# A hybrid decoder layer: plain last iteration of the down projection, own places for the last h forms, and queries split at another unit

## The chip, the cores and the metric

The kernel runs on one core of one Trainium2 chip. The metric is the device time of one execution in microseconds (us). The program is launched once, all inputs lie in device memory (HBM) when the time starts, and the output is written back to it.

## What is computed

One decoder layer on 512 tokens of width 2048, in fp32. Cut to what matters here:

```python
h = rms_norm(x, g_mix_pre);  proj = h @ w_in
c_q, c_kv, k_r, sq, sk, sv = split(proj)       # 512, 512, 64, 1024, 128, 128
out_a = mla_attention(...)                     # 8 heads, dense causal
out_b = swa_attention(sq, sk, sv, sinks, bias) # 16 heads of 64, window 128, 2 key heads
x = x + rms_norm(concat(out_a, out_b) @ w_o, g_mix_post)
h = rms_norm(x, g_ffn_pre)
ff = (silu(h @ w_gate) * (h @ w_up)) @ w_down  # d_ff = 5632
x = x + rms_norm(ff, g_ffn_post)
```

## The kernel before

**Split operands.** Every fp32 product is made of three matmuls: an operand a is split into a rounded high part (written by ScalarE as an activation with Copy) and a low part (VectorE: the source minus the high part), and a·b becomes hi·hi + hi·lo + lo·hi, accumulated in PSUM. So each operand costs ScalarE one pass and VectorE one pass before TensorE may start.

**Order of the work.** The engines follow lists written out by hand, with semaphore waits; nothing is reordered at run time. The stages are the input projection, sliding-window attention in 16 units (four groups of four heads, four query blocks each), latent attention, output projection, gate and up projection in 11 rounds, down projection in 12 iterations, and the last norm and residual.

**Sliding-window units.** In each `window(s)` TensorE does the scores of unit s, the transposes of unit s-3 and the values of unit s-4. The queries of head group g are split into `qs[g % 2]`: ScalarE in `split_queries_hi` (line 907), VectorE in `split_queries_lo` (line 1414). For groups 2 and 3 the two halves are done in units 1 and 2 of the group before on ScalarE (line 941), and one step after that on VectorE (line 1455: at the ends of windows 6, 7 and 10, 11). TensorE waits for both halves in front of the scores of windows 8 and 12 (line 2004).

**Strassen-Winograd.** Gate/up and down projection are done with 7 products in place of 8 for each 2x2 block. In the down projection an iteration is one chunk of the inner dimension (2, 4, 4, 4, 4, 4 pairs of 128 rows) and one half (`cb`) of each output block. Product n = 7·it + f_ takes the weight form `weights_form(f_)` (sums made in place by VectorE, line 1801), a ring slot n % 4 for its high and low part (lines 1237 and 1828), and the h form f_. With 4 pairs it is 2·4·3 = 24 matmuls, with 2 pairs 12. Its 128x1024 result in PSUM pair (n + 1) % 4 is copied (n < 14, line 1242) or added by VectorE (line 1840) into the accumulator `y[f_]`. ScalarE's `form_hi(n)` waits for product n-4, because of the ring.

**The h forms.** The activations h of a round are transposed and summed into 7 forms. Each form is split into a staging place (`h_stage`, two places used in turn; lines 1171 and 1736) and stored to `h_forms` in HBM (line 672), from where `fetch_h` (lines 662 and 666) loads them by chunk. A place is free again when its store has landed (line 1170). The forms of round 10, the last one, are made during products 5 to 12 of the down projection.

```python
if m >= 2:
    act.wait_ge(h_out[m % 2], 16 * (m // 2))              # 1170, ScalarE
nc.scalar.activation(h_stage[m % 2][:, :, 0, :], h_source(i), ACT.Copy)
```

**SP's queue.** All loads and stores of this stage are issued by SP in one order: weights after `d_lo`, h stores after `h_lo`, h loads after `d_done` (lines 721 to 750).

**The end.** In the last two iterations (10 and 11) the seven accumulators of a half are combined: GpSimd adds y0 to y5, y0 to y2, y2 to y1, y1 to y4 and y2 to y6 (`add_into`, line 823), and VectorE adds twice (lines 1845 and 1847), waiting for GpSimd. ScalarE squares the four output blocks (line 1249), VectorE multiplies by the gain (line 1856). After the last product VectorE adds it row block by row block (`late_piece`, line 1921), then for rows 0-1, 2 and 3 forms the inverse root (`y_rstd`, lines 1332 to 1336 and 1895), and adds to x1: the first half by VectorE (line 1912), most of the second by ScalarE's scale (line 1287) and GpSimd's add (line 842). SP stores the rows (lines 755 to 759).

Of the kernel before, what the change touches and what calls it, by code (L numbers as in the profile page):

```python
# [31 lines left out]
ALU = mybir.AluOpType  # L32
# [84 lines left out]
def build(nc, x, positions, g_mix_pre, w_in, g_cq, g_ckv, w_uq, w_ukv, sinks, rel_bias, w_o,  # L117
          g_mix_post, g_ffn_pre, w_gate, w_up, w_down, g_ffn_post, buckets, inv_freq, out):
    ctx = ExitStack()
    with ctx:  # L120
# [111 lines left out]
        h_stage = [sb(f"h_stage{i}", kb, [P, 2, 2, 256], F32R) for i, kb in enumerate((48, 214))]  # L232
        xs = [sb(f"xs{i}", kb, [P, 2, 512]) for i, kb in enumerate((48, 214))]
# [13 lines left out]
        g_row = sb("g_row", 142, [P, D])  # L247
# [8 lines left out]
        h_forms = nc.dram_tensor("h_forms", (7, P, FF_PAIRS, 512), F32, kind="Internal").ap()  # L256
        x1_dram = nc.dram_tensor("x1_dram", (TB, P, D), F32, kind="Internal").ap()
# [22 lines left out]
        y_pool = sem("y_pool")  # L280
# [17 lines left out]
        h_out = [sem(f"h_out{i}") for i in range(2)]  # L298
        slot_in = [[sem(f"w{i}{h}_in") for h in "ab"] for i in range(3)]
# [17 lines left out]
        h_in = [sem(f"h_in{f}") for f in range(7)]  # L317
        g_row_in = sem("g_row_in")
# [3 lines left out]
        d_first = sem("d_first")  # L322
# [5 lines left out]
        y_based = sem("y_based")  # L328
        y_mixed = sem("y_mixed")
        y_sq = sem("y_sq")  # L330
        y_scaled = sem("y_scaled")
# [174 lines left out]
        PRODUCTS = 7 * ITERS  # L506
# [27 lines left out]
        def y_part(t, half):  # L534

            return ((y[5], y[4]), (y[6], y[3]))[t // 2][half][:, t % 2, :]

# [46 lines left out]

        def h_source(i):

            return (h_s34[:, :, :], ht[:, 2, :, :], h_s2[:, :, :], ht[:, 3, :, :], ht[:, 1, :, :], ht[:, 0, :, :],
                    h_s34[:, :, :])[i]
# [19 lines left out]
        def _(sp_):  # L608
# [41 lines left out]
            def forms_stored(pairs):  # L650
                forms = 7 * ((pairs + 1) // 2)
                sp_.wait_ge(h_out[0], 16 * ((forms + 1) // 2))
                sp_.wait_ge(h_out[1], 16 * (forms // 2))

# [14 lines left out]
            def store_form(b, i):  # L669
                m = 7 * b + i  # L670
                sp_.wait_ge(h_lo, m + 1)
                sp_.dma_start(h_forms[H_FORM[i], :, 2 * b:2 * b + 2, :],
                              f(h_stage[m % 2][:, :, :, :]).rearrange("p j h n -> p j (h n)")
                              ).then_inc(h_out[m % 2], 16)
# [14 lines left out]
            for b in range(ROUNDS):  # L689
                for f_ in range(7):  # L690
                    for v in range(4):
                        if v % 2 and f_ in (3, 4, 5, 6):
# [3 lines left out]
                            elif b + 1 < ROUNDS:  # L696
# [5 lines left out]
                                else:  # L702
                                    load(b + 1, "b22", v // 2)
                        if b and (f_, v) in STORE_AT:
# [16 lines left out]
            for n in range(PRODUCTS + 3):  # L721
# [13 lines left out]
                elif it + 1 == ITERS and f_ in (1, 3, 4, 5):  # L735
                    sp_.wait_ge(d_lo, n + 1)
                    t = (1, 3, 4, 5).index(f_)
                    sp_.dma_start(x1_row[t][:, :], x1_dram[t]).then_inc(x1_in[t], 16)
                elif it + 1 == ITERS and f_ == 2:
                    sp_.wait_ge(d_done, PRODUCTS - 6)  # L740
                    sp_.dma_start(g_row[:, :], g_ffn_post.broadcast_to([P, D])).then_inc(g_row_in, 16)
# [6 lines left out]
                if done >= 0 and done // 7 % 2 and done // 14 + 1 < len(CHUNKS):  # L748
                    sp_.wait_ge(d_done, done + 1)
                    fetch_h(done // 14 + 1, done % 7)  # L750

            for t in range(TB):
                sp_.wait_ge(y_ready, t + 1)
                w = shared(t).stop
                sp_.dma_start(out_v[t][:, 0:1024], x1_row[t][:, 0:1024]).then_inc(y_out, 16)
                if w < 1024:
                    sp_.dma_start(out_v[t][:, 1024 + w:D], x1_row[t][:, 1024 + w:D]).then_inc(y_out, 16)
                sp_.wait_ge(y_pool, t + 1)
                sp_.dma_start(out_v[t][:, 1024:1024 + w], x1_row[t][:, 1024:1024 + w]).then_inc(y_out, 16)
            sp_.wait_ge(y_out, 16 * (2 * TB + 1))  # L760
# [1599 lines left out]
```

## Time and profile before

| | |
|---|---|
| time before, median of 3 runs | 2010.66 us (2010.12 to 2011.25) |
| the profiled execution's own time | 2008.88 us |
| its span, first to last instruction | 2007.1 us |
| mean granted TensorE clock | 0.976 |
| TensorE busy / VectorE / ScalarE / GpSimd | 95% / 75% / 45% / 5% |

The span is the traced part of an execution; the 1.78 us around it are not traced. TensorE is busy nearly all the time, so the stretches in which it waits are what can be won.

### The profile page before, as it was taken

The page shows a single profiled execution, that of the slowest core. Times are in us where ns is not written, and L with a number is a line of the kernel's source. Part 1 is how long each engine was busy: PE and PEld are TensorE (multiplying, and loading weights), DVE is VectorE, ACT ScalarE, POOL GpSimd, SP SyncE. Part 2 cuts the span into 40 slices and gives each one's busy share as a digit, 9 for nine tenths or more (in the row PEclk, how much of TensorE's full clock was granted, in tenths as well). Part 3 has the DMA queues.
Part 4 walks back from the last instruction along what each step waited for, and adds up shares of the span by engine and source line. Part 5 has one row for each costly group of instructions (what it writes and reads, how often), then busy time and mean ns, then how long its engine had stood idle before and what let it go on. Part 6 is the DMA issues. An engine that isn't in the chain of part 4 may idle for free. (4 is left out here: it accounts for less than half of the span.)

```text
span 2007.1 us, 22078 instructions
## 1 busy us (share of the span) xinstructions
PE 1901.0 (95%) x8706; PEld 1573.9 (78%) x8706; DVE 1504.6 (75%) x1623; ACT 900.7 (45%) x1212; POOL 109.3 (5%) x63
## 2 busy tenths in 40 slices
PE   8999989999995799999999999999999899999994
PEld 6888778888884688888888888888887688888873
DVE  5762576663226878988988888889887788888887
ACT  5322474453225644454544545545545533333332
POOL 1110130000002000000000000000000000000034
PEclk9999999999997899999999999999999999999997
DMA  8433201115413153462552642733715854644732
GB/s 241 123 97 93 84 12 58 58 64 189 147 64 126 43 168 97 145 220 92 171 180 93 209 147 101 236 116 126 241 64 210 327 219 172 258 183 174 271 125 105
DMA packets 194388, 293.32 MB, mean 146 GB/s; under 512 B 7187, under 2 KB 140396, under 8 KB 188524
## 3 DMA queue, kind: packets, MB, share of 16 engines
q1 hardware_dynamic: 191248, 285.24, 41.7%
q10 hardware_dynamic: 3036, 6.66, 1.1%
q8 instruction: 69, 1.13, 0.2%
q14 instruction: 35, 0.29, 0.0%
HBM read 243.09 MB, written 51.93 MB: 147 GB/s over the span
## 5 line engine op out<-in xcount | busy, mean ns | idle before, releaser
L2277 PE MATMUL pair<-unit_hi,xf 128*128 128x512 f32 x1232 | 488.6, 397 | 24.8 <-DVE unit_lo L1672 24.8
L2279 PE MATMUL pair<-unit_hi,xf 128*128 128x512 f32 x1232 | 483.5, 392 | 0.0
L2278 PE MATMUL pair<-unit_lo,xf 128*128 128x512 f32 x1232 | 483.3, 392 | 0.0
L2277 PEld LDWEIGHTS pair<-unit_hi,xf 128*128 128x128 f32 x1232 | 233.8, 190 | 73.6 <-issue 23.4
L2279 PEld LDWEIGHTS pair<-unit_hi,xf 128*128 128x128 f32 x1232 | 233.6, 190 | 49.9
L2278 PEld LDWEIGHTS pair<-unit_lo,xf 128*128 128x128 f32 x1232 | 234.2, 190 | 47.7
L2331 PE MATMUL pair<-ring_hi,hfs 128*128 128x512 f32 x528 | 207.1, 392 | 7.9 <-DVE ring_lo L1828 7.1
L2332 PE MATMUL pair<-ring_lo,hfs 128*128 128x512 f32 x528 | 206.4, 391 | 0.0
L2333 PE MATMUL pair<-ring_hi,hfs 128*128 128x512 f32 x528 | 206.4, 391 | 0.0
L446 DVE TENSOR_TENSOR wlo<-raw,whi 128x2048 fp32r<-128x2048 f32 (+2 forms) x47 | 96.7, 2064 | 111.0 <-ACT whi L439 111.0
L439 ACT ACTIVATE whi<-raw 128x2048 fp32r<-128x2048 f32 (+2 forms) x47 | 80.9, 1729 | 181.5 <-PE pair L602 173.0
L1237 ACT ACTIVATE ring_hi<-w_b 128x2048 fp32r<-128x2048 f32 (+1 forms) x60 | 105.3, 1772 | 124.7 <-DVE w_b L1808 56.5
L1828 DVE TENSOR_TENSOR ring_lo<-w_b,ring_hi 128x2048 fp32r<-128x2048 f32 (+1 forms) x60 | 132.1, 2202 | 14.5 <-ACT ring_hi L1237 14.5
L2331 PEld LDWEIGHTS pair<-ring_hi,hfs 128*128 128x128 f32 x528 | 99.8, 189 | 30.7 <-DVE ring_lo L1828 8.9
L600 PE MATMUL pair<-act_hi,whi 128*128 128x512 f32 x304 | 120.4, 396 | 0.0
L1840 DVE TENSOR_TENSOR y<-y,pair 128x1024 f32<-128x1024 f32 x69 | 84.1, 1218 | 47.2 <-PE pair L2333 47.2
L602 PE MATMUL pair<-act_hi,wlo 128*128 128x512 f32 x304 | 118.4, 390 | 0.0
L601 PE MATMUL pair<-act_lo,whi 128*128 128x512 f32 x304 | 118.4, 389 | 0.0
L2333 PEld LDWEIGHTS pair<-ring_hi,hfs 128*128 128x128 f32 x528 | 99.7, 189 | 20.9
L2332 PEld LDWEIGHTS pair<-ring_lo,hfs 128*128 128x128 f32 x528 | 99.7, 189 | 20.5
L823 POOL TENSOR_TENSOR y<-y,y 128x1024 f32<-128x1024 f32 x10 | 35.7, 3582 | 1304.8 <-DVE y L1840 1304.5
L600 PE MATMUL pair<-whi,mixt_hi 128*128 128x512 f32 x256 | 99.8, 390 | 0.0
(342 smaller groups left out, 3440.8 us busy)
## 6 DMA issues: line engine op xcount, KB each, us to landing
w_b<-in_w_down SPq DMA_DIRECT2D x40, 1024.0 KB, 5.1
h_forms<-h_stage SPq DMA_DIRECT2D x77, 512.0 KB, 5.2
hfs<-h_forms SPq DMA_DIRECT2D x30, 1024.0 KB, 7.3
raw<-in_w_in SPq DMA_DIRECT2D x19, 1024.0 KB, 5.8
raw<-in_w_o SPq DMA_DIRECT2D x16, 1024.0 KB, 5.0
w0a<-in_w_gate SPq DMA_DIRECT2D x15, 512.0 KB, 3.7
w0a<-in_w_up SPq DMA_DIRECT2D x15, 512.0 KB, 5.7
w0b<-in_w_gate SPq DMA_DIRECT2D x15, 512.0 KB, 3.9
```

The source lines that it names most:

```text
L446: last = nc.vector.tensor_tensor(dst, src, f(hi), ALU.subtract)
L600: nc.tensor.matmul(out_ap, a[0], b[0], start=first, stop=False)
L601: nc.tensor.matmul(out_ap, a[0], b[1], start=False, stop=False)
L602: return nc.tensor.matmul(out_ap, a[1], b[0], start=False, stop=last)
L1237: nc.scalar.activation(ring(ring_hi, n), weights_form(f_, np_), ACT.Copy).then_inc(d_hi, 1)
L1828: nc.vector.tensor_tensor(ring(ring_lo, n), weights_form(f_, np_), f(ring(ring_hi, n)), ALU.subtract).then_inc(d_lo, 1)
L2277: nc.tensor.matmul(dst, a[0], w[0], start=kk == 0, stop=False)
L2278: nc.tensor.matmul(dst, a[0], w[1], start=False, stop=False)
L2279: last = nc.tensor.matmul(dst, a[1], w[0], start=False, stop=kk == 7)
L2331: nc.tensor.matmul(dst, a[0], b[0], start=k == 0, stop=False)
L2332: nc.tensor.matmul(dst, a[0], b[1], start=False, stop=False)
L2333: last = nc.tensor.matmul(dst, a[1], b[0], start=False, stop=k == np_ - 1)
```

## The change

In three parts: (1) the queries of groups 2 and 3 are split one unit earlier. (2) In round 10 the h forms 1 to 6 get six places of their own; for rounds 9 and 10 the unchanged block A21 is also stored, as an eighth form. (3) The last iteration of the down projection (4 inner pairs, half cb = 1) is done as 8 plain block products. The accumulators are combined by VectorE alone, those of half 1 before the plain blocks are added.

```diff
+        h_last = [sb(f"h_last{i}", 4 * i, [P, 2, 2, 256], F32R) for i in range(6)]
+        hf_a21 = sb("hf_a21", 150, [P, 4, 2, 256], F32R)
-        PRODUCTS = 7 * ITERS
+        PLAIN = 7 * (ITERS - 1)
+        FORMS = PLAIN + 4
+        PLAIN_BLOCKS = ((0, 0, 0), (1, 0, 1), (2, 1, 0), (3, 1, 1))
+        def plain_form(n):
+            return (w_b11, w_b21, w_b12, w_b22)[n - PLAIN]
+        COMBINE = ((5, 0), (2, 0), (4, 2), (4, 1), (3, 2), (6, 3), (3, 1))
+        EXTRA = FIRST_PAIR[-2] // 2
+        def h_place(b, i):
+            m = h_form(b, i)
+            if b == ROUNDS - 1 and i > 0:
+                return h_last[i - 1], h_last_out
+            return h_stage[m % 2], h_out[m % 2]
...
@@ SP, down projection
+                if n == 5:
+                    store_form(ROUNDS - 1, -1)
...
+                if done == PLAIN - 6:
+                    sp_.wait_ge(d_done, done + 1)
+                    forms_stored(FF_PAIRS)
+                    sp_.dma_start(f(hf_a21[:, :, :, :]).rearrange("p j h n -> p j (h n)"),
+                                  h_a21).then_inc(a21_in, 16)
...
             for t in range(TB):
-                sp_.wait_ge(y_ready, t + 1)
...
+                for half in range(2):
+                    sp_.wait_ge(y_ready, 2 * t + half + 1)
+                    a = slice(1024 * half, 1024 * half + 1024)
+                    sp_.dma_start(out_v[t][:, a], x1_row[t][:, a]).then_inc(y_out, 16)
@@ GpSimd
-            for it in (ITERS - 2, ITERS - 1):
...
-                nc.gpsimd.tensor_tensor(a, a, y_part(t, 1)[:, shared(t)], ALU.add).then_inc(y_pool, 1)
@@ ScalarE
-                    if n in (1, 2) and 1 <= gh < 3:
+                    if n in (0, 1) and 1 <= gh < 3:
                         act.wait_ge(s_qk, 4 * gh)
-                        split_queries_hi(gh + 1, n - 1)
+                        split_queries_hi(gh + 1, n)
...
             def form_of_h_hi(b, i):
...
-                if m >= 2:
-                    act.wait_ge(h_out[m % 2], 16 * (m // 2))
-                nc.scalar.activation(h_stage[m % 2][:, :, 0, :], h_source(i), ACT.Copy).then_inc(h_hi, 1)
+                place, stored = h_place(b, i)
+                if stored is not h_last_out and m >= 2:
+                    act.wait_ge(stored, 16 * (m // 2))
+                nc.scalar.activation(place[:, :, 0, :], h_source(i), ACT.Copy).then_inc(h_hi, 1)
...
@@ form_hi(n)
                 elif n == 16:
                     act.wait_ge(d_done, 14)
+                elif n == 14:
+                    act.wait_ge(d_done, 11)
+                    act.wait_ge(h_last_out, 16 * 6)
                 else:
                     act.wait_ge(d_done, n - 3)
...
+            def plain_hi(n):
+                act.wait_ge(d_done, n - 3)
+                act.wait_ge((b11_in, b21_in, b12_in, b22_in)[n - PLAIN], 16 * ITERS)
+                nc.scalar.activation(ring(ring_hi, n), plain_form(n)[:, :, :], ACT.Copy).then_inc(d_hi, 1)
@@ VectorE
-                if 4 < s < 12 and s % 4 >= 2:
-                    split_queries_lo(s // 4 + 1, s % 4 - 2)
+                if 4 < s < 12 and s % 4 in (1, 2):
+                    split_queries_lo(s // 4 + 1, s % 4 - 1)
...
+                if n == 5:
+                    form_of_h_lo(ROUNDS - 1, -1)
                     form_of_h_sum(ROUNDS - 1, 1)
...
+                if n in (PLAIN - 4, PLAIN - 3, PLAIN - 1):
+                    combine(1, (PLAIN - 4, PLAIN - 3, PLAIN - 1).index(n))
+            plain_lo(FORMS - 1)
+            for k in range(3, 7):
+                combine(1, k)
+            for k in range(4):
+                combine(0, k)
+            dve.wait_ge(g_row_in, 16)
+            block_add(0)
+            for half in range(2):
+                y_times_gain(0, half, 0)
+                y_times_gain(1, half, 0)
+            for k in range(4, 7):
+                combine(0, k)
+            y_times_gain(0, 0, 1)
+            y_times_gain(1, 0, 1)
+            block_add(1)
+            for half in range(2):
+                y_times_gain(2, half, 0)
+                y_times_gain(3, half, 0)
...
+            y_rstd(0, 2, squared(1, 1, 1), 8, 4, 12, lambda: late_gains(0, 2, (1,)))
+            row_add(2, 0)
             y_residual(0)
             y_residual(1)
-            y_rstd(2, 3, 15, 9, 5, lambda: late_gain(2))
...
+            row_add(2, 1)
+            y_rstd(2, 3, squared(2, 1, 1), 9, 5, 14, lambda: late_gains(2, 3, (0, 1)))
+            row_add(3, 0)
             y_residual(2)
...
+            row_add(3, 1)
+            y_rstd(3, 4, squared(3, 1, 1), 10, 6, 16, lambda: late_gains(3, 4, (0, 1)))
             y_residual(3)
@@ TensorE
-            for n in range(PRODUCTS):
+            for n in range(PLAIN):
...
+            for n in (PLAIN, PLAIN + 1):
+                pe.wait_ge(*evictions(n - 4))
+                for inner in range(2):
+                    pe.wait_ge(d_lo, PLAIN + 2 * (n - PLAIN) + inner + 1)
+                    for t in range(2):
+                        last = plain_part(n, t, inner)
+                last.then_inc(d_done, 1)
+            pe.wait_ge(*evictions(PLAIN - 1))
+            pe.wait_ge(a21_in, 16)
+            for t in range(2):
+                for n in (PLAIN + 2, PLAIN + 3):
+                    for inner in range(2):
+                        last = plain_part(n, t, inner)
+                    last.then_inc(d_done, 1)
```

`combine` adds one accumulator to another (128x1024), `block_add` adds a plain block of rows 0-1, `row_add` one row block of rows 2-3 from PSUM; `plain_part` is 12 matmuls. The six places `h_last` lie at 0 to 24 KB of a partition, where ring slots 2 and 3 of the high and low parts lie too; slot 2 is first written by `form_hi(14)`.

## Rows read from the trace of the kernel before

**Rows 1.** Waits of TensorE, whole kernel: us in total, times, longest us
```profile
PE pair L2331 <- DVE ring_lo L1828: 14.4, 5, 4.6
```

**Rows 2.** TensorE's timeline, windows 8 and 12: start, us, instruction, [idle before]
```profile
257.25 0.38 PE L600 MATMUL pair<-kpad_hi,qs_hi 128*128 128x256 f32 x1 [2.91 <-DVE qs_lo L1414]
...
275.79 0.57 PE L600 MATMUL pair<-kpad_hi,qs_hi 128*128 128x256 f32 x1 [2.77 <-DVE qs_lo L1414]
```

**Rows 3.** Timeline, VectorE, the second query split of group 2
```profile
255.17 2.03 DVE L1414 TENSOR_TENSOR qs_lo<-sq,qs_hi 128x512 fp32r<-128x512 f32 x1
```

**Rows 4.** Stretches: us; busy PE, PEld, DVE, ACT, POOL; clock, DMA share, GB/s
```profile
257.00:262.00 5.00, 4.75 (x24) 4.46 (x25) 2.88 (x15) 3.08 (x12) 1.89 (x1) 0.68 0.11 40
...
1800.00:1900.00 100.00, 100.00 (x443) 82.81 (x442) 86.74 (x50) 36.07 (x19) 0.56 (x1) 1.00 0.59 223
1928.00:1934.00 6.00, 5.49 (x13) 4.33 (x14) 6.00 (x5) 3.36 (x5) 0.00 (x0) 0.50 0.00 0
```

**Rows 5.** Timeline, TensorE between products 9, 10 and 14
```profile
1566.04 0.39 PE L2333 MATMUL pair<-ring_hi,hfs 128*128 128x512 f32 x1
...
1571.05 0.80 PE L2331 MATMUL pair<-ring_hi,hfs 128*128 128x512 f32 x1 [4.63 <-DVE ring_lo L1828]
...
1587.43 0.50 PE L2331 MATMUL pair<-ring_hi,hfs 128*128 128x512 f32 x1 [0.53 <-DVE ring_lo L1828]
```

**Rows 6.** Timeline, ScalarE: h form 6 of round 10, and form_hi(14)
```profile
1578.28 0.63 ACT L1171 ACTIVATE h_stage<-h_s 128x512 fp32r<-128x512 f32 x1 [5.25 <-DMA h_forms<-h_stage]
...
1582.52 1.91 ACT L1237 ACTIVATE ring_hi<-w_b 128x2048 fp32r<-128x2048 f32 x1
```

**Rows 7.** Transfers of SP issued at 1571.03, 1574.74, 1557.6: KB, us to landing
```profile
w_b<-in_w_down SPq DMA_DIRECT2D x1, 1024.0 KB, 5.9
...
hfs<-h_forms SPq DMA_DIRECT2D x1, 1024.0 KB, 12.2
...
h_forms<-h_stage SPq DMA_DIRECT2D x1, 512.0 KB, 2.6
```

**Rows 8.** The same of the h stores issued at 1571.63 and 1581.74, each
```profile
h_forms<-h_stage SPq DMA_DIRECT2D x1, 512.0 KB, 6.5
```

**Rows 9.** VectorE: timeline of two low parts; line 1828, ns min/median/max
```profile
1569.77 1.23 DVE L1828 TENSOR_TENSOR ring_lo<-w_b,ring_hi 128x1024 fp32r<-128x1024 f32 x1 [5.81 <-ACT ring_hi L1237]
1570.91 0.69 DVE L1736 TENSOR_TENSOR h_stage<-ht,h_stage 128x512 fp32r<-128x512 f32 x1
...
L1828 DVE TENSOR_TENSOR ring_lo<-w_t,ring_hi x24: 1217/2287/2290, 1541.1 to 1971.3; 128x2048 fp32r<-128x2048 f32 x20, 128x1024 fp32r<-128x1024 f32 x4
```

**Rows 10.** Timeline, TensorE around products 76 and 83
```profile
1924.62 0.39 PE L2333 MATMUL pair<-ring_hi,hfs 128*128 128x512 f32 x1
1928.52 0.79 PE L2331 MATMUL pair<-ring_hi,hfs6a 128*128 128x512 f32 x1 [3.50 <-DVE ring_lo L1828]
...
1973.63 0.79 PE L2331 MATMUL pair<-ring_hi,hfs6a 128*128 128x512 f32 x1 [3.85 <-DVE ring_lo L1828]
...
1981.52 0.39 PE L2333 MATMUL pair<-ring_hi,hfs6b 128*128 128x512 f32 x1
```

**Rows 11.** Timeline, VectorE in the tail
```profile
1923.77 1.22 DVE L1845 TENSOR_TENSOR y<-y,y 128x1024 f32<-128x1024 f32 x1 [6.07 <-POOL y L823]
...
1976.95 6.11 DVE L1856 TENSOR_TENSOR y<-y,g_row 128x512 f32<-128x512 f32 x10
...
1984.44 0.16 DVE L1332 RECIPROCAL small<-small 128x2 f32<-128x2 f32 x1
...
1986.03 2.48 DVE L1912 SCALAR_TENSOR_TENSOR x_row<-y,small,x_row 128x1024 f32<-128x1024 f32 x2
...
1994.09 0.69 DVE L1921 TENSOR_TENSOR y<-y,pair 128x512 f32<-128x512 f32 x1
...
1995.88 0.15 DVE L1895 TENSOR_REDUCE small<-ss 128x1 f32<-128x4 f32 x1
```

**Rows 12.** Timeline, SP: the last store
```profile
2003.48 0.79 SPq L759 DMA_DIRECT2D out_dram<-x_row  x1
```

More of the change, by code:

```diff
@@ L719, in _ @@
             fetch_h(0, 5)
-            for n in range(PRODUCTS + 3):
+            for n in range(PLAIN + 3):
                 it, f_ = divmod(n, 7)
@@ L1903, in y_rstd @@
                 dve.wait_ge(rstd_ready, n_rstd)
+                dve.wait_ge(gained, n_gained)
             def y_residual(t):
                 dve.wait_ge(x1_in[t], 16)
-                parts = [(0, slice(0, 1024))]
-                if shared(t).stop < 1024:
-                    parts.append((1, slice(shared(t).stop, 1024)))
-                for half, a in parts:
-                    dst = x1_row[t][:, half * 1024 + a.start:half * 1024 + a.stop]
-                    last = nc.vector.scalar_tensor_tensor(out=dst, in0=y_part(t, half)[:, a], scalar=rstd[:, t:t + 1],
-                                                          in1=dst, op0=ALU.mult, op1=ALU.add)
@@ L1928, in _, with late_gains @@
-            y_rstd(0, 2, 14, 8, 4, lambda: y_times_gain(0, 0, 1, 14))
-            late_piece(2)
-            dve.wait_ge(gained, 7)
+                for half in range(2):
+                    dst = x1_row[t][:, half * 1024:half * 1024 + 1024]
+                    nc.vector.scalar_tensor_tensor(out=dst, in0=y_part(t, half), scalar=rstd[:, t:t + 1], in1=dst,
+                                                   op0=ALU.mult, op1=ALU.add).then_inc(y_ready, 1)
+            def late_gains(t0, t1, halves_):
+                for t in range(t0, t1):
+                    for half in halves_:
+                        y_times_gain(t, half, 1)
@@ L2338, in _, with plain_part @@
                     h_transposes(ROUNDS - 1, 3)
+            def plain_part(n, t, inner):
+                c = len(CHUNKS) - 1
+                _, rows, right = PLAIN_BLOCKS[n - PLAIN]
+                form = PLAIN + 2 * right + inner
+                dst = bank[2 * product_pair(n) + t]
+                for k in range(CHUNKS[c]):
+                    if (rows, inner) == (1, 0):
+                        a = [hf_a21[:, k, h, P * t:P * t + P] for h in range(2)]
+                    else:
+                        a = [hf(c, (0, 5, 6)[rows + inner], k, h, t) for h in range(2)]
+                    b = [ring(r, form)[:, k, :] for r in (ring_hi, ring_lo)]
+                    first, end = (inner, k) == (0, 0), (inner, k) == (1, CHUNKS[c] - 1)
+                    nc.tensor.matmul(dst, a[0], b[0], start=first, stop=False)
+                    nc.tensor.matmul(dst, a[0], b[1], start=False, stop=False)
+                    last = nc.tensor.matmul(dst, a[1], b[0], start=False, stop=end)
+                return last
+            for n in (PLAIN, PLAIN + 1):
[12 more added lines that the diff above has]
+                    last.then_inc(d_done, 1)
 _INS = ["x", "positions", "g_mix_pre", "w_in", "g_cq", "g_ckv", "w_uq", "w_ukv", "sinks", "rel_bias", "w_o",
```

248 lines of the change are left out of this document (116 added, 132 removed).

## The prediction

> **What bounds the kernel now.** I read the granted clock and the busy shares first: TensorE is busy for 95% of the span, so only its waits, its restarts at the lower clock and what follows its last matmul can be won. The list of its waits comes next, and the timeline around each wait that the change touches. (1) In front of windows 8 and 12 it waits 2.91 and 2.77 us for the queries' low parts [rows 2]. (2) The down projection has 14.4 us of waits for `ring_lo` [rows 1]: 4.63 us before product 10 and 0.53 us before product 14 stand in [rows 5], another lies between. Behind them stands ScalarE, held by a store of an h form: 5.25 us before form 6 [rows 6]. (3) In front of product 76, and again before product 83, TensorE waits 3.50 and 3.85 us, because VectorE, which has to make the low part of product 76, sat 6.07 us until GpSimd's adds were done [rows 10, 11]. (4) From the last matmul, 1981.5 + 0.2 = 1981.7 [rows 10], to the end of the span at 2007.1 it is 25.4 us.
>
> Two prices are used throughout. At full clock a matmul of 512 columns costs 100 us / 443 = 0.226 us [rows 4], so a product of 24 costs 5.4 us. After a wait of 3.5 us and more the granted clock is 0.50, the lower of the two levels (1.2 GHz), and 13 matmuls take the 5.5 us of 1928.5 to 1934 [rows 4], 0.42 us each. Product 76 so took from 1928.52 to about 1937.0, some 3.0 us more than 5.4.
>
> **Part 1, the queries.** Nothing is added; two ScalarE and two VectorE passes per group come one window earlier. Their second VectorE pass began at 255.17, took 2.03 us, and TensorE started at 257.25 [rows 2, 3]. What it needs otherwise for window 8 (the maxima of window 6) is long there, so both waits go: 5.7 us. The clock of 0.68 behind the first [rows 4] gives back something too: 24 matmuls there are in part at the lower level, up to 1.5 us for each wait, so the upper bound is 8.5. The lower bound is 0: VectorE's 2 x (1.4 to 2.0) us of passes have not gone, and where it has no idle time in windows 5, 6, 9 and 10 they only move. Following the two lists through windows 5 to 12, the next thing late is VectorE's reciprocal and GpSimd's 1.9 us multiplication behind it [rows 4], by less than 1 us. I take 5.0 us off.
>
> **Part 2, the h forms.** ScalarE no longer waits for stores, so products 10 to 13 (12 matmuls each) can follow product 9 at once: 1566.04 + 0.23 + 48 x 0.226 = 1577.1 [rows 5], where product 14 started at 1587.43. That is 10.3 us to be had. But a new wait stands in front of `form_hi(14)`: all six new places must have been stored, since ring slot 2 lies on them. When is the sixth store in? VectorE had emptied its list at 1564.0 (1569.77 less 5.81) [rows 9]. The eighth form adds one pass of 0.7 us and delays that to 1564.7; then come four passes of 1.2 us (three low parts and a sum) and three h passes of 0.6 to 0.7 [rows 9], so form 6 is ready at 1571.1 and its store is issued. In SP's order it stands behind weights b11 (issued at 1566.0, after the low part of product 10), store 4, an h load, weights b22, store 5 and another h load. Before, these landed in the order of their issue: b11 at 1571.03 + 5.9 = 1576.9, store 4 at 1578.1, the second h load at 1574.74 + 12.2 = 1586.9 and store 6 at 1581.74 + 6.5 = 1588.2 [rows 7, 8], although a lone store takes 2.6 us [rows 7]. That is 4.5 MB in 11.3 us behind b11, 2.5 us for each MB. In the new order b11 lands 5.9 us after 1566.0, or up to 1 us later behind the two stores and b12 ahead of it: 1572.5. Store 6 follows 11.3 us later, at 1583.8. Then 1.9 us of ScalarE [rows 6] and 2.3 us of VectorE [rows 9] for the four-pair slot, with 0.2 us between: product 14 starts at 1588.2 to 1588.4, 0.9 us later than before. What was several waits has become one of 11 us, behind which the clock is low: 3.0 us more, as at product 76. So this part costs 4 us. Its bounds are a gain of 10.3 and a loss of 6 (one transfer of 1 MB more ahead of the store, 2.5 us). Work with one answer: the extra form of round 9 (ScalarE 0.6, VectorE 0.7 us, one store) lies in the gate/up rounds, where both wait for TensorE in front of the same units, so 0, and 0.7 if that cover is gone; the wait before the last unit of the gate/up projection, for a store of round 9, stays, since that round keeps the two places.
>
> The Trainium skill, page "DMA: Bandwidth & Descriptors", section "Queues, rings and completion order", says that descriptors are consumed in ring order on each DMA engine, but that completion is not first in, first out per issuing engine. By its first half and the landings above the sum stands; if the second half let the store finish early, this would be rival A.
>
> **Part 3, the last iterations.** Without GpSimd's adds VectorE is never held: the low part of product 76 is ready by 1918, so the product starts at 1924.62 + 0.23 = 1924.85 and ends at 1930.3, where it ended at 1937.0: 6.7 us. Then four blocks of 48 matmuls replace 7 products of 24: 192 x 0.226 = 43.4 us, end at 1973.7. Eight matmul groups in place of seven cost 5.4 us of this, and the second wait with its low clock (4.0 + 3.0 us) is gone. TensorE so ends at 1973.7 and not at 1981.7: 8.0 us. Operands: weights are raw, so the four splits (2.2 to 2.3 us each) need no sums and end by 1936, the first use of the last being at 1946; A21 is loaded after product 71 into the place of form 1, the gain after 72, the x1 rows after the splits, all more than 10 us ahead.
>
> Does VectorE keep up? From 1936.1 its list is 11 adds of accumulators and 2 blocks at 1.13 to 1.25, 10 gain passes at 0.6 (6.11 for 10) [rows 11], so 21.4 us: 1957.5. Then the norm of rows 0-1 (two passes of 0.15, 2 x 0.6, and 1.0 from the reciprocal at 1984.44 to the row add 0.6 before 1986.03), a row add 0.6, four residual passes of 1.2 (2.48 for two), a row add, the norm of row 2 (1.2 until its square, 0.3, 1.2, 1.0), a row add and two residuals: 1972.9. The last row add can start at 1973.7 + 0.3 = 1974.0, so VectorE is in time by about 1 us. From there: 1.8 us to the reduction (1994.09 to 1995.88) [rows 11], 0.3, two gain passes 1.2, inverse root 1.0, two residual passes 2.5: 1980.8. The last store then takes 3.6 us to the end of the span (from 2003.48 to 2007.1) [rows 12]: 1984.4. After the last matmul 10.7 us are left of 25.4: no GpSimd add, no scale pass, and no VectorE instruction stretched by GpSimd. Part 3: 2007.1 - 1984.4 = 22.7 us off. Bounds: 18 (each of the 11 adds 0.2 us longer and one more wait for ScalarE's squares) and 24.
>
> **Sum.** 5.0 - 4.0 + 22.7 = 23.7 us off a span of 2007.1: 1983.4, and 1985.2 for the profiled execution, whose own time was 1.8 us above its span. That execution lies 1.8 us under the median, so off the median 2010.66 it is 1987.0.
>
> **Rivals.** (A) The sixth store lands early, because the transfers ahead of it are spread over more time or finish after it: at 1571.1 + 2.8 it is in at 1574, and product 14 starts at 1574 + 0.2 + 1.9 + 2.3 = 1578.4, a gain of 9.0 with no low clock. Then 2010.66 - 5.0 - 9.0 - 22.7 = 1974.0. For it: few transfers are issued before 1566. Against it: 5 MB ahead of the store in 5 us, and landings in order [rows 7, 8]. (B) VectorE is the bound of the windows, and part 1 brings nothing: 1992.0. For it: a split took 2.03 us beside GpSimd [rows 3]; against it: the wait was for the split itself. (C) VectorE is late in the tail: its margin is 1 us, and any more goes through to the end; 5 us more give 1992. (D) Slower: the plain blocks run at the lower clock. They are one run of 192 matmuls; if a short wait in front of each of them, for `d_lo` or an eviction, brought the clock of 0.50 [rows 4], they would cost 192 x (0.42 - 0.226) = 37 us more, 2010.66 - 23.7 + 37 = 2024. It decides from 23.7 / 0.194 = 122 matmuls at that level. Against it: every operand of the blocks is ready 5 us and more ahead, and 443 matmuls ran in 100 us at a clock of 1.00 [rows 4].
>
> **How the numbers follow.** The forecast gets 0.55, A 0.18, B 0.12, C 0.12, D 0.03. The range takes in A and the bounds of B and C: 1973 to 1994. A measurement of this kernel can tell 0.2%, 4 us, from no change. Only D, or all bounds at their bad ends and more, gives less than 4 us: faster 0.94, within it 0.03, slower 0.03.
>
> **What would show it.** Right: no wait for `qs_lo` before windows 8 and 12 (the one at window 4 stays); ScalarE's `form_hi(14)` idle for about 13 us until a store, one wait of 10 to 11 us of TensorE in front of product 14 and 15 slow matmuls; no wait from product 14 to the end, a clock of 1.00 from product 76 on, TensorE's last matmul 9 us earlier in the span (8.0 + 5.0 - 4.0), and 10.7 us after it. Wrong: product 14 without a wait (A), VectorE back to back through windows 5 to 12 with TensorE waiting for it in every one (B), VectorE's last `row_add` later than 0.5 us after the last matmul (C), a clock of 0.50 in the blocks (D).

## The result, and the profile of the changed kernel

The changed kernel takes 1984.3 us (median of 4 runs, 1983.0 to 1986.1), the kernel before 2010.4 us in the same session (2006.2 to 2011.3): a ratio of 0.9875 with a 95% interval of 0.9858 to 0.9892. The forecast was 1987.0 us. The profiled execution has a time of 1983.6 us and a span of 1981.3 us, where the kernel before had 2007.1: 25.8 us less, where the sum of the prediction was 23.7.

**The queries.** TensorE's timeline in window 4 and in windows 8 and 12 (start, us, instruction, idle time before it and what ended it), in the order of time:

```profile
238.89 0.38 PE L638 MATMUL pair<-kpad_hi,qs_hi 128*128 128x256 f32 x1 [3.31 <-DVE qs_lo L1450]
...
254.90 0.28 PE L638 MATMUL pair<-kpad_hi,qs_hi 128*128 128x256 f32 x1
...
257.95 0.39 PE L638 MATMUL pair<-spt_hi,vpad_hi 128*128 128x256 f32 x1 [1.29 <-ACT mix_s L949]
...
270.17 0.28 PE L638 MATMUL pair<-kpad_hi,qs_hi 128*128 128x256 f32 x1
...
273.22 0.39 PE L638 MATMUL pair<-spt_hi,vpad_hi 128*128 128x256 f32 x1 [1.29 <-ACT mix_s L949]
```

The wait for `qs_lo` is left in window 4 alone. The scores of windows 8 and 12 begin without one, and the granted clock behind window 8's start is 1.00 where [rows 4] had 0.68 (columns as there). Behind each a new wait of 1.29 us has come, for ScalarE's `mix_s` (a copy of attention results out of PSUM). All waits for it sum to 5.5 us, where they were 3.4.

```profile
255.00:260.00 5.00, 3.71 (x27) 3.26 (x26) 4.46 (x21) 4.54 (x19) 3.44 (x2) 1.00 0.38 105
```

**The h forms.** TensorE, ScalarE and VectorE around product 14, one fence for each engine's timeline:

```profile
1541.22 0.47 PE L2385 MATMUL pair<-ring_hi,hfs 128*128 128x512 f32 x1 [0.78 <-ACT ht L1187]
...
1555.82 0.50 PE L2385 MATMUL pair<-ring_hi,hfs 128*128 128x512 f32 x1 [0.46 <-DVE ring_lo L1869]
...
1572.19 0.39 PE L2387 MATMUL pair<-ring_hi,hfs_first 128*128 128x512 f32 x1
...
1583.09 0.79 PE L2385 MATMUL pair<-ring_hi,hfs 128*128 128x512 f32 x1 [10.51 <-DVE ring_lo L1869]
```

```profile
1578.80 1.91 ACT L1270 ACTIVATE ring_hi<-w_b 128x2048 fp32r<-128x2048 f32 x1 [12.61 <-DMA h_forms<-h_last]
```

```profile
1580.74 2.29 DVE L1869 TENSOR_TENSOR ring_lo<-w_b,ring_hi 128x2048 fp32r<-128x2048 f32 x1 [11.03 <-ACT ring_hi L1270]
```

Read backwards: TensorE stands for VectorE, which stands for ScalarE, which stands 12.61 us for the stores of the new places. 1541.22 is the start of product 3; before, it was 1546.73. SP's timeline tells when that store was issued, and the two answers on transfers below it (KB, us from issue to landing) are those of weights b11, issued at 1560.40, and of the sixth store, issued at 1565.79:

```profile
1560.40 0.38 SPq L686 DMA_DIRECT2D w_b<-in_w_down  x1
1561.00 0.59 SPq L718 DMA_DIRECT2D h_forms<-h_last  x1
1561.70 0.39 SPq L703 DMA_DIRECT2D hfs<-h_forms  x1
1562.32 0.38 SPq L686 DMA_DIRECT2D w_b<-in_w_down  x1
1562.92 0.38 SPq L718 DMA_DIRECT2D h_forms<-h_last  x1
1563.41 0.38 SPq L703 DMA_DIRECT2D hfs<-h_forms  x1
1565.79 0.32 SPq L718 DMA_DIRECT2D h_forms<-h_last  x1
```

```profile
w_b<-in_w_down SPq DMA_DIRECT2D x1, 1024.0 KB, 7.0
...
h_forms<-h_last SPq DMA_DIRECT2D x1, 512.0 KB, 12.9
```

So b11 landed at 1567.4 and the store at 1578.7: 11.3 us for the 4.5 MB between them. The stretches show the full rate ahead of product 14 (DMA share 1.02, 429 GB/s, TensorE without a matmul) and the low clock behind the wait (0.53):

```profile
1574.00:1582.00 8.00, 0.00 (x0) 0.00 (x0) 1.26 (x1) 3.20 (x3) 0.00 (x0) 0.72 1.02 429
1582.00:1588.00 6.00, 4.91 (x12) 3.90 (x13) 6.00 (x4) 5.01 (x4) 0.00 (x0) 0.53 0.50 206
```

**The last iterations.** Behind the wait at 1583.09 no further wait of TensorE is listed. VectorE's timeline of the tail, and the last matmul of TensorE behind it:

```profile
1929.44 4.49 DVE L1874 TENSOR_TENSOR ring_lo<-w_b,ring_hi 128x2048 fp32r<-128x2048 f32 x2
1933.84 9.66 DVE L1891 TENSOR_TENSOR y<-y,y 128x1024 f32<-128x1024 f32 x8
1943.42 1.22 DVE L1897 TENSOR_TENSOR y<-y,pair 128x1024 f32<-128x1024 f32 x1
...
1971.82 0.69 DVE L1902 TENSOR_TENSOR y<-y,pair 128x512 f32<-128x512 f32 x1 [1.61 <-PE pair L2406]
1973.30 0.16 DVE L1961 TENSOR_REDUCE small<-ss 128x1 f32<-128x4 f32 x1 [0.79 <-ACT junk L1285]
...
1975.72 2.48 DVE L1975 SCALAR_TENSOR_TENSOR x_row<-y,small,x_row 128x1024 f32<-128x1024 f32 x2
```

```profile
1971.39 0.39 PE L2406 MATMUL pair<-ring_hi,hfs6b 128*128 128x512 f32 x1
```

TensorE's stretch ahead of it runs at the full clock:

```profile
1920.00:1970.00 50.00, 50.00 (x222) 41.42 (x221) 44.56 (x56) 16.41 (x35) 0.00 (x0) 1.00 0.34 128
```

The eight accumulator adds of the second line take 1.2 us each and wait for nobody; before, VectorE stood 6.07 us for GpSimd's adds in front of one of its own [rows 11]. VectorE had 1.61 us to spare before the last row add. From the last matmul's end (1971.4 + 0.2) to the span's end are 9.7 us, where there were 25.4.

### The profile page after: what moved, and what is told of

Same layout as the page of the kernel before. It is cut to its first block, busy times and chain, and to the rows that moved or that the text cites. A ratio compares the mean times of both kernels' runs of the same rounds, so it can differ in the third digit from the quotient of the medians.

```text
span 1981.3 us, 22101 instructions
## 1 busy us (share of the span) xinstructions
PE 1897.1 (96%) x8730; PEld 1572.1 (79%) x8730; DVE 1489.2 (75%) x1629; ACT 892.5 (45%) x1207; POOL 64.2 (3%) x49
## 4 chain that ended last, share of the span: by engine, by line
PE 89%; DVE 5%; ACT 3%; DMA 2%; issue 1%; DVEq 0%; SPq 0%; ACTq 0%
PE pair L2331 14%; PE pair L2333 14%; PE pair L2332 14%; PE pair L638 8%; PE pair L640 8%; PE pair L639 8%; PE pair L2385 6%; PE pair L2386 6%; PE pair L2387 6%; PE pair L2342 1%; PE pair L2406 1%; PE pair L2404 1%; PE pair L2405 1%; DMA h_forms<-h_last 1%; ACT sp L963 1%
## 5 line engine op out<-in xcount | busy, mean ns | idle before, releaser
L2385 PE MATMUL pair<-ring_hi,hfs 128*128 128x512 f32 x480 | 188.4, 393 | 11.7 <-DVE ring_lo L1869 11.0
L2386 PE MATMUL pair<-ring_lo,hfs 128*128 128x512 f32 x480 | 187.6, 391 | 0.0
L2387 PE MATMUL pair<-ring_hi,hfs 128*128 128x512 f32 x480 | 187.5, 391 | 0.0
L1270 ACT ACTIVATE ring_hi<-w_b 128x2048 fp32r<-128x2048 f32 (+1 forms) x55 | 95.9, 1759 | 132.8 <-DVE w_b L1849 56.9
L1869 DVE TENSOR_TENSOR ring_lo<-w_b,ring_hi 128x2048 fp32r<-128x2048 f32 (+1 forms) x55 | 115.1, 2093 | 14.5 <-ACT ring_hi L1270 14.4
L2385 PEld LDWEIGHTS pair<-ring_hi,hfs 128*128 128x128 f32 x480 | 90.6, 189 | 32.2 <-DVE ring_lo L1869 12.4
L1881 DVE TENSOR_TENSOR y<-y,pair 128x1024 f32<-128x1024 f32 x63 | 76.8, 1219 | 51.2 <-PE pair L2387 51.2
L2387 PEld LDWEIGHTS pair<-ring_hi,hfs 128*128 128x128 f32 x480 | 90.6, 189 | 19.0
L2386 PEld LDWEIGHTS pair<-ring_lo,hfs 128*128 128x128 f32 x480 | 90.7, 189 | 18.6
L639 PE MATMUL pair<-wlo,mixt_hi 128*128 128x512 f32 x256 | 99.6, 389 | 0.0
```

What stands on the lines that cost most here:

```text
L639: nc.tensor.matmul(out_ap, a[0], b[1], start=False, stop=False)
L1270: nc.scalar.activation(ring(ring_hi, n), weights_form(f_, np_), ACT.Copy).then_inc(d_hi, 1)
L1869: nc.vector.tensor_tensor(ring(ring_lo, n), weights_form(f_, np_), f(ring(ring_hi, n)), ALU.subtract).then_inc(d_lo, 1)
L2385: nc.tensor.matmul(dst, a[0], b[0], start=k == 0, stop=False)
L2386: nc.tensor.matmul(dst, a[0], b[1], start=False, stop=False)
L2387: last = nc.tensor.matmul(dst, a[1], b[0], start=False, stop=k == np_ - 1)
```

## Experiments

The runs of three later sessions are compared with the kernel before on the same chip (medians 2008.9, 2009.7 and 2008.3 us) and with the changed kernel's 1984.3 of the first session; it was not run again in the later ones. Differences of times between two variants of the changed kernel carry 2 to 3 us of uncertainty; those inside one profile are read closer. Where the text gives a stretch between two products for several profiles, it is read from the start of the first matmul of each.

**Part 1 undone.** The queries split at their old units, all else as changed.

```diff
-                    if n in (0, 1) and 1 <= gh < 3:
+                    if n in (1, 2) and 1 <= gh < 3:
...
-                if 4 < s < 12 and s % 4 in (1, 2):
+                if 4 < s < 12 and s % 4 >= 2:
```

> The kernel after, with the queries of groups 2 and 3 split at their old units. Theory (part 1 is worth its two waits on TensorE, 5.5 us, and nothing later gives them back): 1984.3 + 5.5 = 1989.8 us, TensorE waits 2.8 to 2.9 us for qs_lo before windows 8 and 12 as in the kernel before, and the matmul in front of product 3 of the down projection starts 5.5 us later in the span. Rival (VectorE is the bound of the windows, and the shift seen comes from somewhere else): 1984 to 1986 us.

Measured: 1988.6 us (1987.5 to 1989.9), ratio 0.9895 [0.9882, 0.9908], span 1987.2. The waits are back:

```profile
258.58 0.58 PE L638 MATMUL pair<-kpad_hi,qs_hi 128*128 128x256 f32 x1 [2.91 <-DVE qs_lo L1450]
...
276.99 0.39 PE L638 MATMUL pair<-kpad_hi,qs_hi 128*128 128x256 f32 x1 [2.79 <-DVE qs_lo L1450]
```

Part 1 is worth 4.3 us by the medians and 5.9 by the spans; product 3 starts 6.6 us later (1547.82), where 5.5 were expected. The stretch of the windows itself says more than one pair. From the wait of 3.31 us in front of window 4 to a wait of 1.1 us for `mix_s` that all profiles have some 16 us behind the start of window 12, it is 48.3 us in six profiles with the new split and 49.4 in a seventh, and 51.7, 53.1, 54.8 and 54.8 us in the four with the old one: 3.4 to 6.4 us of gain, 5.1 by the means. Rival B (VectorE bounds the windows) is out.

**Part 2's places undone.** All h forms in the two staging places, no wait for the stores in `form_hi(14)`, and SP's own waits for the stores counted to match; the eighth form stays.

```diff
-            if b == ROUNDS - 1 and i > 0:
+            if False:
                 return h_last[i - 1], h_last_out
...
@@ form_hi(n)
-                elif n == 14:
-                    act.wait_ge(d_done, 11)
-                    act.wait_ge(h_last_out, 16 * 6)
```

> The kernel after, with all h forms of round 10 in the two staging places again, the eighth form kept, and no wait for the last stores before form_hi(14). Theory 1 (the own places brought one long wait, 10.5 us with a low clock behind it, in place of waits of 7.1 us with one low clock, and that is the loss of 3.3 us in this stretch): without them the old waits return, 1984.3 - 3.3 = 1981.0 us. Theory 2 (the eighth form puts one more store into the chain of two places, so with two places each later form comes 2 to 3 us later): 1983 to 1986 us, TensorE's waits before products 10 to 14 sum to 9 to 12 us. In both, no wait of over 1.5 us stands before product 14 itself.

Measured: 1984.9 us (1983.4 to 1986.2), ratio 0.9877 [0.9864, 0.9890]: no difference from the changed kernel that can be told. The one wait has become three:

```profile
1554.86 0.50 PE L2380 MATMUL pair<-ring_hi,hfs 128*128 128x512 f32 x1 [2.29 <-DVE ring_lo L1864]
...
1569.05 0.79 PE L2380 MATMUL pair<-ring_hi,hfs 128*128 128x512 f32 x1 [4.13 <-DVE ring_lo L1864]
...
1579.33 0.80 PE L2380 MATMUL pair<-ring_hi,hfs 128*128 128x512 f32 x1 [2.98 <-DVE ring_lo L1864]
```

They stand in front of products 7, 10 and 12. Their sum is 9.4 us against 10.5 + 0.5 (in front of products 10 to 14 alone it is 7.1, where the expectation had 9 to 12), and first matmuls of 0.79 and 0.80 us show the low clock behind two of them. From the start of product 3 to that of product 15 it is 50.6 us here, 49.8 in the next run, which has two places too, and 49.6, 49.1 and 48.8 in three profiles with own places. With the eighth form in the chain of two places, own places win about 1 us here, too little to be told from the times, as long as one wait stands for all six stores.

The same stretch shows a price that no run was made for: with two places and no eighth form it is 46.3 us (the kernel before) and 47.4 (the next run but one, the same program up to there). The eighth form so costs some 3 us in two places. What it costs with own places is not known, since part 3 needs it and no run leaves it out.

**Part 3 alone.** Both edits together; the eighth form stays.

> Part 3 alone (with the eighth form, which it needs): queries and places as in the kernel before. Theory: the last iteration and its tail are worth 23.6 us whatever stands before: 2010.4 - 23.6 = 1986.8 us, plus 0 to 5 us for the eighth form in the chain of two places. From product 76 on the trace should be that of the kernel after, shifted: last matmul to the end of the span 9.7 us, no wait of TensorE from product 20 on. Rival (the parts lean on each other, for instance a store queue that the places shorten): over 1992 us.

Measured: 1989.8 us (1986.4 to 1991.4), ratio 0.9899 [0.9885, 0.9914], span 1986.7. By the spans that is 20.4 us under the kernel before and 5.4 over the changed one: the part that carries the change is the tail.

**The kernel before without GpSimd's adds.** All combining adds of the last two iterations on VectorE, in the same order; the seven products of the last iteration stay.

```diff
-            for it in (ITERS - 2, ITERS - 1):
...
+            def add_into(dst, src, cb):
+                a, b = y_of(dst, cb), y_of(src, cb)
+                nc.vector.tensor_tensor(a, a, b, ALU.add).then_inc(y_based, 1)
...
+                if last_it >= 0 and f_ == 2:
+                    dve.wait_ge(*evictions(n))
+                    add_into(2, 0, cb)
...
```

> The kernel before, with one difference: the ten accumulator adds of the last two iterations are done by VectorE in its own order in place of GpSimd; still 84 Strassen products, still GpSimd's add of x1. It tells 'without GpSimd' apart from 'plain last iteration'. Theory: TensorE's waits of 3.5 and 3.9 us and the two low clocks behind them go (14 us), but VectorE has 32 of 38 us of an iteration filled already and takes 6 us more, so the last two products come some 2 us late, and its list behind the last low part (33.5 us to the end of the span) stays: 2000 to 2004 us, 8 us faster than before. So about 15 us of the 23.6 would be the plain blocks with their short tail. Rival (GpSimd's adds were the whole cost): 1987 to 1990 us. Rival (VectorE full, the waits only change their name): 2008 to 2012 us.

Measured: 2002.4 us (1999.8 to 2006.9), ratio 0.9967 [0.9956, 0.9979], span 1998.0. The waits of 3.50 and 3.85 us in front of products 76 and 83 [rows 10] are gone. A new one of 1.76 us stands in front of product 82, since VectorE now makes four adds one after the other ahead of its low part; the second line is the start of product 83:

```profile
1958.73 0.50 PE L2329 MATMUL pair<-ring_hi,hfs 128*128 128x512 f32 x1 [1.76 <-DVE ring_lo L1811]
...
1964.58 0.50 PE L2329 MATMUL pair<-ring_hi,hfs6a 128*128 128x512 f32 x1
...
1969.93 0.39 PE L2331 MATMUL pair<-ring_hi,hfs6b 128*128 128x512 f32 x1
```

TensorE's last matmul is 11.6 us earlier than in [rows 10] (2.5 us of it were there by product 3 already), the span only 9.1: from that matmul to the end it is still 28 us. Moving the adds is worth 6.5 us by the medians. The spans of this one pair differ by 9.1, but the stretch from product 20 to the end, which leaves out most of what the edit doesn't touch, by 7.7. The rest of part 3's 23.6 us, some 16, comes with the plain blocks and the tail written for them. They cost TensorE one block product more (5.4 us) and pay by leaving nothing to combine behind it.

Not all of the 16 us is the plain blocks' own, and no run has the one without the other. In the tail of this run, as in that of the kernel before, three VectorE instructions that run beside GpSimd's adds of x1 take 2.58, 2.10 and 2.10 us, where the like of them take 0.7, 0.16 and 0.16; that is some 6 us on VectorE's list, and the changed kernel has no such adds there. One of the three:

```profile
1982.32 2.10 DVE L1316 TENSOR_TENSOR small<-small 128x1 f32<-128x1 f32 x1
```

**Three semaphores for the six stores.** The one wait of `form_hi(14)` is cut into what lies under each reader.

```diff
-        h_last_out = sem("h_last_out")
+        h_last_out = [sem(f"h_last_out{i}") for i in range(3)]
...
-                return h_last[i - 1], h_last_out
+                return h_last[i - 1], h_last_out[(i - 1) // 2]
...
-                    act.wait_ge(h_last_out, 16 * 6)
+                    act.wait_ge(h_last_out[0], 16 * 2)
...
             def form_lo(n):
+                if n in (14, 15):
+                    dve.wait_ge(h_last_out[n - 13], 16 * 2)
```

> The kernel after, with three semaphores for the stores of the six places in place of one: ScalarE's form_hi(14) waits only for the stores of forms 1 and 2 (on which the high part of ring slot 2 lies), VectorE's form_lo(14) for those of forms 3 and 4, form_lo(15) for those of forms 5 and 6. Theory 1 (the wait of 10.5 us is for the sixth store alone, which lands at 1578.7 behind the transfers issued ahead of it, in the order of issue): product 14 starts where product 13 ends, at about 1572.8 in place of 1583.1; product 15 would start at 1578.2 but for the store at 1578.7 and 2.3 us of VectorE, so at about 1581.3: a wait of 3 us in place of 10.5, with some microseconds of low clock behind it or none. Gain on the kernel after 7 to 10 us: 1975 to 1977. Theory 2 (the wait has other legs: the weights or the h loads of product 14 or 15 land no earlier than that store): product 14 or 15 still waits until about 1583, and the gain is under 5 us.

Measured: 1976.6 us (1975.1 to 1978.8), ratio 0.9836 [0.9822, 0.9849]: 7.7 us under the changed kernel. VectorE's and TensorE's timelines, and the stretch behind product 15's start:

```profile
1580.88 2.29 DVE L1872 TENSOR_TENSOR ring_lo<-w_b,ring_hi 128x2048 fp32r<-128x2048 f32 x1 [3.44 <-DMA h_forms<-h_last]
```

```profile
1583.23 0.79 PE L2388 MATMUL pair<-ring_hi,hfs 128*128 128x512 f32 x1 [3.70 <-DVE ring_lo L1872]
```

```profile
1583.00:1589.00 6.00, 5.77 (x14) 4.56 (x15) 6.00 (x5) 3.53 (x2) 0.00 (x0) 0.51 1.02 408
```

Product 14 follows 13 without a wait; product 15 stands 3.70 us for the same store, and the clock still falls to 0.51. (This execution reached product 3 at 1542.71, 1.5 us later than the changed kernel. The sixth store landed at 1580.9, 2.2 us later than the 1578.7 expected: 1.5 by that start, and the rest because it took 13.6 us from its issue, where it took 12.9.)

**The sixth store issued earlier.** As before, and in SP's list the h load (1,1) comes behind the store.

```diff
-                if done >= 0 and done // 7 % 2 and done // 14 + 1 < len(CHUNKS):
+                if done >= 0 and done // 7 % 2 and done // 14 + 1 < len(CHUNKS) and done != 8:
                     sp_.wait_ge(d_done, done + 1)
+                    if done == 9:
+                        fetch_h(1, 1)
                     fetch_h(done // 14 + 1, done % 7)
```

> As the one before, and SP issues the sixth store ahead of the h load (1,1) of 1 MB that stood before it. Theory 1: the store lands 2.5 us earlier (2.5 us for each MB ahead of it), at about 1576.2, the low part of product 15 ends at 1578.7 and TensorE waits under 1 us in front of it: 10 to 12 us faster than the kernel after, 1972 to 1975. Theory 2: the DMA rings are at their full rate there, so what is moved back (the h load) is late next and product 15 waits for it instead: no gain on the kernel with three semaphores.

Measured: 1972.2 us (1972.0 to 1974.9), ratio 0.9819 [0.9805, 0.9832].

```profile
1576.58 2.29 DVE L1874 TENSOR_TENSOR ring_lo<-w_b,ring_hi 128x2048 fp32r<-128x2048 f32 x1 [0.22 <-DMA h_forms<-h_last]
```

```profile
1579.07 0.47 PE L2390 MATMUL pair<-ring_hi,hfs 128*128 128x512 f32 x1 [0.75 <-DVE ring_lo L1874]
```

```profile
1579.00:1585.00 6.00, 5.93 (x26) 4.95 (x27) 6.00 (x4) 4.01 (x3) 0.00 (x0) 1.00 1.01 419
```

VectorE waits 0.22 us for the store in place of 3.44, TensorE 0.75 us in place of 3.70, and the clock stays at 1.00: 26 matmuls in the 6 us where there were 14. What was moved back, the h load, is not late. Against the run with the semaphores alone, in the same session, this is 4.4 us by the medians.

**The order alone.** The changed kernel with that edit and its one semaphore, to price the landing by itself.

> The kernel after with the change of order alone (the sixth store ahead of the h load (1,1)), one semaphore as it was. Theory of landings in the order of issue at 2.5 us for each MB: form_hi(14) starts at 1576.3 in place of 1578.8, and product 14 2.5 us earlier: 1981 to 1982. Theory that a store from SBUF lands by its own rate whatever is ahead of it: no change, 1984.

Measured: 1982.5 us (1980.8 to 1984.6), ratio 0.9865 [0.9851, 0.9878]; 1.8 us under the changed kernel, and just above the 1981 to 1982 that were expected. The times alone would not settle that it is faster. The profile does:

```profile
1576.22 1.91 ACT L1272 ACTIVATE ring_hi<-w_b 128x2048 fp32r<-128x2048 f32 x1 [9.90 <-DMA h_forms<-h_last]
```

```profile
1580.51 0.79 PE L2387 MATMUL pair<-ring_hi,hfs 128*128 128x512 f32 x1 [7.80 <-DVE ring_lo L1871]
```

ScalarE is released 2.58 us earlier than at 1578.80, with product 3 at 1541.34 in place of 1541.22, so 2.7 us earlier by that clock. From issue to landing the store takes 10.2 us in place of 12.9; between the two kernels with three semaphores it is 10.5 in place of 13.6. One MB less ahead of the store is 2.7 to 3.1 us, a little over the 2.5 of the theory; what the rest is stays open. The kernel of the run before differs from this one by the three semaphores alone and was run in the same session: 1972.2 against 1982.5, so the finer wait is worth 10.3 us with the store issued early.

**A wait that the change left.** In the changed kernel ScalarE also sits 7.49 us for a store of round 9, held behind eight transfers that SP issues in one block, and TensorE 2.83 us in front of the last unit of gate/up. Here, on top of the three semaphores and the new order, four of the eight are issued at a later step:

```diff
                             fetch_h(0, 0)
                             fetch_h(0, 1)
+                        if b == ROUNDS - 1 and (f_, v) == (6, 2):
                             fetch_w(0, 0, 1, 1, w_b22, b22_in)
                             fetch_h(0, 2)
                             fetch_w(0, 0, 1, 0, w_b21, b21_in)
                             fetch_h(0, 6)
```

> As the one before, and four of the eight transfers that SP issues in one block at step (5,1) of round 10 (weights b22 and b21, h loads of forms 2 and 6, about 2 MB) are issued at step (6,2), behind the stores of round 9. In the kernel after, ScalarE sits 7.49 us until 1523.5 for such a store, behind which TensorE waits 2.83 us for unit_lo in front of the last unit of gate/up. Theory: the store lands 3 to 5 us earlier, that wait goes, 3 to 4 us faster than the kernel before it in this list. Against it: the moved loads are needed by products 1 and 2, some 10 us after their issue, and may be late there; then it is no faster.

Measured: 1967.7 us (1966.6 to 1968.8), ratio 0.9790 [0.9777, 0.9804]. ScalarE's wait, first in the changed kernel, then here:

```profile
1523.47 0.63 ACT L1199 ACTIVATE h_stage<-h_s 128x512 fp32r<-128x512 f32 x1 [7.49 <-DMA h_forms<-h_stage]
```

```profile
1518.20 0.63 ACT L1203 ACTIVATE h_stage<-h_s 128x512 fp32r<-128x512 f32 x1 [2.42 <-DMA h_forms<-h_stage]
```

ScalarE has the place 5.3 us earlier, TensorE no longer waits there, and product 3 starts at 1535.96 in place of 1541.51 in the kernel without this edit. By the medians that is 4.6 us less than in the kernel without this edit, where 3 to 4 were expected, and the moved loads were not late. This is the fastest version found: 16.6 us under the changed kernel, 42 under the one before.

**VectorE made late in the tail.** The changed kernel with four more passes.

```diff
+            for k in range(4):
+                link(nc.vector.tensor_tensor(w_t2[:, 0:2, :], w_t2[:, 0:2, :], w_t2[:, 2:4, :], ALU.add))
             y_rstd(0, 2, squared(1, 1, 1), 8, 4, 12, lambda: late_gains(0, 2, (1,)))
```

> The kernel after with four more passes of VectorE over 128x1024 elements, of 1.2 to 1.3 us each, in the tail, just ahead of the norm of rows 0-1 (they write a buffer that nothing reads any more). It measures the margin that the forecast gave VectorE in the tail (about 1 us; the trace of the kernel after shows 1.61 us of idle time in front of the last row add). Theory (VectorE is in time by 1.6 us and no wait ahead of the last row add takes up more of the delay): 4.9 to 5.2 us of passes less 1.6, so 3.3 to 3.6 us slower than the kernel after, 1987.5 to 1988.5, the wait of VectorE for the last block gone and its last row add 3.3 to 3.6 us later after the last matmul. Rival (ScalarE's squares and the stores have a chain of their own that sets the end): under 2 us slower, 1984 to 1986.

Measured: 1990.0 us (1987.8 to 1991.5), ratio 0.9907 [0.9890, 0.9924], span 1987.0.

```profile
1957.69 4.99 DVE L1984 TENSOR_TENSOR w_t<-w_t 128x1024 f32<-128x1024 f32 x4
...
1977.45 0.68 DVE L1902 TENSOR_TENSOR y<-y,pair 128x512 f32<-128x512 f32 x1
```

```profile
1973.72 0.39 PE L2408 MATMUL pair<-ring_hi,hfs6b 128*128 128x512 f32 x1
```

Five us of passes put the last row add 3.73 us behind the start of the last matmul, where it was 0.43: 3.30 us later, 5.0 less 1.6 to 1.7. Inside the profile the theory holds to 0.1 us. The time went up by 5.7, above the expected 1987.5 to 1988.5; 2.3 us of that stood already at the last matmul (1973.72 against 1971.39), and 2.8 at product 3, ahead of anything that this edit touches. In the profiled execution that part is a difference between executions, not an effect of the passes. The median of the four lies as high; whether for the same reason is not shown, since the others were not profiled.

## Why the prediction was right

It named 1987.0 us and 23.7 us of gain; measured were 1984.3 and 25.8 in the span. Point by point:

- **Part 1** (5.0 forecast): product 3 starts 5.5 us earlier, at 1541.22 for 1546.73. The mechanism is as described: both waits for `qs_lo` are gone and no other takes their full length. What came next was not what was named (VectorE's reciprocal and GpSimd's multiplication, under 1 us): both windows got a wait of 1.29 us for ScalarE's `mix_s`, and by all waits for it 2.1 us of the gain went, most of what the clock gave back. Taking 5.0 between bounds of 0 and 8.5 was a choice. Product 3 moves by 2.5 to 2.8 us between executions of kernels that are the same up to there, so the agreement of the one pair is in part luck; over all profiles the windows give 5.1 us by the means, from 3.4 to 6.4.
- **Part 2** (a loss of 4.0): this pair of traces gives 3.3. The waits up to product 14 cost 1.2 us (0.9 forecast): it starts 4.34 us earlier than in [rows 5], with 5.5 in hand. The low clock behind it cost 2.1 us more (3.0 forecast, from product 76, where the wait was shorter): this is the term that was mis-sized. By all profiles the loss is smaller. From product 3 to product 15 it is 46.3 and 47.4 us with the old round 10, and 48.8 to 49.6 in three profiles of the new one: 1.4 to 3.3 us, 2.3 by the means. The landing itself was right: 1583.8 forecast, less the 5.5 us by which product 3 came earlier, is 1578.3, and it came at 1578.7, late by the 0.4 us by which b11 was (1567.4 for 1567.0). What the sum didn't ask is what the eighth form costs without the places: it stands there as a pass of 0.7 us, and in two places it costs some 3. So against the kernel that part 3 needs anyway, own places are no loss, and the 2.3 us are the price of both together. Rival A is out in the changed kernel, and the order-alone run shows why: the store stands behind every transfer issued ahead of it, at 2.5 to 3.1 us for each MB. What rival A promised was there to be had, 9 us plus the clock, but by a finer wait and an order of issue, which the two runs with semaphores and order took.
- **Part 3** (22.7): 25.8 - 5.5 + 3.3 = 23.6. TensorE ends 10.1 us earlier, of which 5.5 - 3.3 = 2.2 are the other parts': 7.9 of its own, for 8.0. How this divides between GpSimd's adds and the plain blocks the prediction did not say; the run without GpSimd's adds gives some 8 and 16 us. Behind the last matmul 25.4 us have become 9.7, for 10.7: from the last row add to the reduction it took 1.5 us for 1.8, and from the end of the last residual (1975.7 + 2.5) to the span's end 3.1 for 3.6. VectorE's margin was 1.6 us for about 1, so rival C did not come; the run with four more passes shows that it would have gone through one for one. Its cover is thin: of two further passes of 1.2 us in this tail 0.8 us would go through to the end.
- **Rival D** (blocks at the lower clock) is out: no wait at all between product 14's and the last matmul at 1971.39, and 222 matmuls in the 50 us from 1920 to 1970, 0.225 us each, which is the full clock.

## What to carry to other kernels

A semaphore that counts a set of transfers makes every reader wait for the last of them; wait for what lies under each reader, and, where the queue is full, price a store by the megabytes that stand ahead of it and not by its own size: here 512 KB took 2.6 us alone and 12.9 us behind the others. Own buffers remove a wait only if nobody soon reuses them, else it moves to the reuse. At the end of a kernel a scheme that saves matmuls but leaves sums to make afterwards can lose to the plain one: compare the time behind the last matmul, too.

## What the runs showed of the hardware

- A small VectorE instruction that starts beside a GpSimd add can be held until it ends. In the kernel before with VectorE's adds, a product of 128x1 elements took 2.10 us where its neighbours took 0.16:

```profile
1987.60 2.37 POOL L825 TENSOR_TENSOR x_row<-x_row,y 128x1024 f32<-128x1024 f32 x1 [3.19 <-ACT y L1270]
1987.69 0.16 DVE L1315 RECIPROCAL small<-small 128x1 f32<-128x1 f32 x1
1987.88 2.10 DVE L1316 TENSOR_TENSOR small<-small 128x1 f32<-128x1 f32 x1
...
1990.02 0.16 DVE L1317 TENSOR_TENSOR small<-small 128x1 f32<-128x1 f32 x1
```

  The GpSimd add ends at 1989.97 and the small product at 1989.98. Not every instruction is held: the reciprocal, which has one tensor as its input where the product has two, starts beside the same add and takes 0.16 us. The changed kernel has no GpSimd instruction in its tail, and none of its small ones is stretched.
- The same wait need not be followed by the same clock. After a wait of 2.91 us the matmul of the next unit came 3.99 us later in the profile of before, and after 2.90 us it came 2.88 us later in the kernel with VectorE's adds, which is the same program up to there; first the profile of before, then the other:

```profile
261.24 0.63 PE L602 MATMUL pair<-kpad_hi,qs_lo 128*128 128x512 f32 x1
```

```profile
257.56 0.39 PE L600 MATMUL pair<-kpad_hi,qs_hi 128*128 128x256 f32 x1 [2.90 <-DVE qs_lo L1397]
...
260.44 0.39 PE L602 MATMUL pair<-kpad_hi,qs_lo 128*128 128x512 f32 x1
```

  That is 1.1 us of the 2.5 by which these two profiles differ at product 3 (1546.73 and 1544.18). A term of that size can't be read off from two single executions; the same stretch in several profiles, as for parts 1 and 2 above, shows how far it moves.
- Behind product 15's wait of 3.70 us the granted clock was 0.51, behind its wait of 0.75 us in the next kernel 1.00: 14 and 26 matmuls in 6 us. The 12 matmuls of difference are worth 12 x 0.226 = 2.7 us, about as much as the wait itself lost in length.
